# A decoder layer in fp32: GpSimd's weight splits wait at two layer norms, and ScalarE multiplies the index scores by their sign

## What is computed

```python
rel = relu(einsum('bthd,bsd->bths', iq, ik))
score = einsum('bths,bth->bts', rel, iw) * idx_scale      # index scores, causal
_, sel = lax.top_k(score, 256)                            # 256 keys for each query
...                                                       # attention over them, and over a window
h = layer_norm(ALPHA * h + mix, ln1_g, ln1_b)             # LN1
c = memory_cross_attention(h, mem, wq, wk, wv, wo)
h = layer_norm(ALPHA * h + c, ln2_g, ln2_b)               # LN2
h = layer_norm(ALPHA * h + square(relu(h @ w_up)) @ w_down, ln3_g, ln3_b)
```

## Time and profile before

| | us |
|---|---|
| median of 3 runs | 1533.02 (1532.31 to 1533.21) |
| the profiled execution | 1530.0 |
| its span in the trace | 1528.2 |
| PE busy | 1458.5 |
| DVE busy | 1088.0 |
| POOL busy | 756.9 |
| ACT busy | 497.6 |

### The profile page before, as it was taken

One profiled execution on the slowest core, in us unless ns is written; L12 is line 12 of the kernel. 1 busy time (PEld: TensorE's weight loads), 2 busy tenths in 40 slices (PEclk: granted clock), 3 DMA queues, 4 the chain that ended last, 5 costly groups with the idle time before them and its releaser, 6 DMA issues.

```text
span 1528.2 us, 21072 instructions
## 1 busy us (share of the span) xinstructions
PE 1458.5 (95%) x7552; PEld 1243.1 (81%) x7552; DVE 1088.0 (71%) x2097; ACT 497.6 (33%) x1044; POOL 756.9 (50%) x583
## 2 busy tenths in 40 slices
PE   6999898999899999989999899999999999999996
PEld 6877788898899988778887688888888888888885
DVE  7568999787977323964418668787777777777857
ACT  3024488888876621122301111111111111111111
POOL 5341357766700033044312367778676777777612
PEclk9999999999999999999999999999999999999999
DMA  6346156655410042121001002020111112020202
GB/s 240 132 163 173 71 193 198 189 167 179 152 29 15 2 171 77 55 84 55 29 28 56 28 28 83 28 79 32 55 55 56 55 32 80 28 83 1 83 28 83
DMA packets 61479, 128.98 MB, mean 84 GB/s; under 512 B 6976, under 2 KB 34112, under 8 KB 53696
## 3 DMA queue, kind: packets, MB, share of 16 engines
q1 hardware_dynamic: 44352, 100.37, 20.0%
q10 hardware_dynamic: 17024, 27.27, 5.0%
HBM read 100.35 MB, written 27.26 MB: 84 GB/s over the span
## 4 chain that ended last, share of the span: by engine, by line
PE 80%; DVE 12%; issue 2%; ACT 2%; DMA 2%; POOL 1%; ACTq 0%; SPq 0%; DVEq 0%; POOLq 0%
PE banks L872 22%; PE banks L874 22%; PE banks L873 22%; PE banks L1078 4%; PE banks L926 2%; PE banks L927 2%; PE banks L1065 2%; DVE h_buf L2126 2%; PE banks L1034 1%; PE banks L1087 1%; DVE bn L2112 1%; DVE act_lo L2105 1%; DMA u_dram<-stage_out 1%; DVE score L1754 1%; DVE h_buf L2135 1%
## 5 line engine op out<-in xcount | busy, mean ns | idle before, releaser
L782 POOL TENSOR_SCALAR w_hi<-raw 128x512 fp32r<-128x512 f32 x156 | 105.3, 703 | 430.2 <-PE banks L874 278.7
L2251 DVE TENSOR_TENSOR h_buf<-h_buf,banks 128x512 f32<-128x512 f32 x320 | 202.6, 678 | 13.2 <-PE banks L874 9.7
L787 POOL TENSOR_TENSOR w_lo<-raw,w_hi 128x512 fp32r<-128x512 f32 x156 | 209.6, 1379 | 0.0
L872 PE MATMUL banks<-act_hi,w_hi 128*128 128x512 f32 x512 | 200.1, 391 | 1.6 <-DVE act_lo L2105 1.6
L873 PE MATMUL banks<-act_lo,w_hi 128*128 128x512 f32 x512 | 199.9, 390 | 0.0
L874 PE MATMUL banks<-act_hi,w_lo 128*128 128x512 f32 x512 | 199.8, 390 | 0.0
L872 PE MATMUL banks<-w_hi,act_hi 128*128 128x512 f32 x384 | 153.4, 399 | 0.0
L872 PE MATMUL banks<-seven_hi,hid_hi 128*128 128x512 f32 x392 | 152.6, 389 | 0.0
L874 PE MATMUL banks<-seven_hi,hid_lo 128*128 128x512 f32 x392 | 152.5, 389 | 0.0
L873 PE MATMUL banks<-seven_lo,hid_hi 128*128 128x512 f32 x392 | 152.5, 389 | 0.0
L874 PE MATMUL banks<-w_hi,act_lo 128*128 128x512 f32 x384 | 150.7, 392 | 0.0
(11 more groups left out here) (222 smaller groups left out, 3513.5 us busy)
## 6 DMA issues: line engine op xcount, KB each, us to landing
raw<-w_down_dram SPq DMA_DIRECT2D x16, 1024.0 KB, 4.8
raw_up<-w_up_dram SPq DMA_DIRECT2D x14, 1024.0 KB, 4.8
q_tile<-qk_dram SPq DMA_DIRECT2D x176, 64.0 KB, 2.9
qk_dram<-q_hi ACTq DMA_DIRECT2D x28, 256.0 KB, 2.1
qk_dram<-roped ACTq DMA_DIRECT2D x28, 256.0 KB, 2.5
x_raw<-x_t_dram SPq DMA_DIRECT2D x8, 512.0 KB, 8.4
raw<-wk_mem_dram SPq DMA_DIRECT2D x4, 1024.0 KB, 5.3
raw<-wv_mem_dram SPq DMA_DIRECT2D x4, 1024.0 KB, 5.7
```

The costliest lines, as they stand in the source:

```text
L782: pool.tensor_scalar(w_hi[s][:, col], source[:, col], 1.0, 1.0, ALU.mult, ALU.mult)\
L787: pool.tensor_tensor(w_lo[s][:, col], source[:, col], w_hi[s][:, col].bitcast(F32), ALU.subtract).then_inc(w_ready, 1)
L872: pe.matmul(dst, lh, rh, start=(first and n == 0), stop=False)
L2251: ins = dve.tensor_tensor(out, out, ring_m[g % 6][:], ALU.add if way > 0 else ALU.subtract)
```

## The change

GpSimd gets two more waits: ahead of chunk C_G+2 it waits until all 8 tiles of LN1 are done (`ln_done` at NT = 8), and ahead of the first two `form_weights` until all 8 of LN2 are done. The multiplication by the sign goes from VectorE's `prepare` to ScalarE, as an activation `Copy` with the sign as its scale, in the same half, behind the ReLUs of that half and ahead of its counts. Two semaphores carry it: `sign_ready` (VectorE to ScalarE) and `flipped` (ScalarE to those who count). The loop on ScalarE takes a half's ReLUs ahead of its counts; no half has both.

```diff
+FLIPS = [INDEX_HALVES[v] - FIRST_TOPK_TILE for v in sorted(INDEX_HALVES)]
@@ GpSimd, weight chunks
                 pool.wait_ge(raw_in[c % 2], 16 * (c // 2 + 1))
+                if c == C_G + 2:
+                    pool.wait_ge(ln_done, NT)
@@ GpSimd, form_weights
                 if x < 2:
+                    pool.wait_ge(ln_done, 2 * NT)
                     chunk_used(pool, C_MLP - 2)
@@ ScalarE, count_scores
                 if BEFORE[q] is None:
+                    act.wait_ge(flipped, FLIPS.index(c) + 1)
                     act.wait_ge(trial_ready, EARLY_TILES.index(c) + 1)
@@ ScalarE
+            def flip_scores(v):
+                c = INDEX_HALVES[v - 1] - FIRST_TOPK_TILE
+                i = FIRST_TOPK_TILE + c
+                act.wait_ge(sign_ready, FLIPS.index(c) + 1)
+                act.activation(score[i][:], score[i][:], ACT.Copy, scale=sign[:, c:c + 1]).then_inc(flipped, 1)
@@ ScalarE, the loop over the halves
+                    for n in index_own(v):
+                        rectify_scores(n)
+                    if v - 1 in INDEX_HALVES:
+                        flip_scores(v)
                     for q in counts_beside_rope(v):
                         count_scores(q)
-                    for n in index_own(v):
-                        rectify_scores(n)
@@ VectorE, prepare
-                signed = then(dve.tensor_scalar(sign[:, col], negative[:, col], -2.0, 1.0, ALU.mult, ALU.add))
+                dve.tensor_scalar(sign[:, col], negative[:, col], -2.0, 1.0, ALU.mult, ALU.add)\
+                    .then_inc(sign_ready, 1)
-                dve.wait_ge(dve_step, signed)
-                flipped = then(dve.tensor_scalar(score[i][:], score[i][:], sign[:, col], None, ALU.mult))
-                dve.wait_ge(dve_step, flipped)
@@ VectorE, narrow_tally
+                    if c not in found_flipped:
+                        found_flipped.add(c)
+                        dve.wait_ge(flipped, FLIPS.index(c) + 1)
```

More of the change, by code:

```diff
@@ L522, in build_layer @@
         kv_hi_done = sem("kv_hi_done")
+        sign_ready, flipped = sem("sign_ready"), sem("flipped")
         stored = sems("stored", 2)
@@ L1812, in prepare @@
                 dve.wait_ge(dve_step, offsets)
-                dve.wait_ge(dve_step, flipped)
                 dve.memset(trial[:, col], SIGN_BIT + (1 << TOP_BIT)).then_inc(trial_ready, 1)
+            found_flipped = set()
             def select_keys():
                 def narrow_tally(c):
+                    if c not in found_flipped:
+                        found_flipped.add(c)
+                        dve.wait_ge(flipped, FLIPS.index(c) + 1)
                     dve.wait_ge(dve_step, set_at[c])
```

## The result

| | before | after |
|---|---|---|
| median of the runs, us | 1532.66 (1526.5 to 1533.21) | 1518.53 (1516.3 to 1518.72) |
| the profiled execution | 1530.0 | 1518.52 |
| its span in the trace | 1528.2 | 1516.0 |
| ratio of the times | | 0.9917 (0.9892 to 0.9941) |

The changed kernel is faster by 14.1 us at the medians; 13.0 were forecast (1520.0). In the profiled executions it is 11.5 us. Measured twice more, the same kernel came out at 0.9905 (0.9887 to 0.9922) and 0.9905 (0.9885 to 0.9924).

What follows compares the result with a forecast made beforehand. TensorE, busy 95% of the span, was taken as the bound, so time is won only where it waits. LN1 6.6 + LN2 4.0 + sign multiplication 2.4 = 13.0 us, from 1533.0 to 1520.0 us, range 1514 to 1526.

Steps and rivals of the forecast that it cites:

- The wait at LN1: At LN1, holding GpSimd's split removes TensorE gaps of 3.8 and 1.0 us and 1.8 us at half clock: 6.6 us.
- What it puts behind itself: GpSimd's later splits at LN1 move by 10 us, with 20 us left before product 24: cost nothing.
- LN2: At LN2, 3.6 of VectorE's 7 us arrive, low parts following ScalarE's rounding: 4.0 us with the clock fallen.
- one of two cases: Behind LN2, TensorE's clock falls (LN2 gives 4.0 us) or stays up (5.7 us; rival 1517.5 us, chance 0.20).
- The sign part: Index stage: multiplication off VectorE gives 0.68, 0.54, 0.4, 0.8 us for tiles 7, 5, 6, 4: 2.4 us.
- VectorE feels it only in its `flush`, behind `rope_first`: Half 18: ScalarE's counts come 0.9 us later, reaching VectorE only there, so TensorE should not feel it: 0 to 0.9 us.
- the sign of being wrong that was named for it: Half 18: a longer wait of VectorE for ScalarE's counts that moves `rope_first` of the next half.
- The prediction's upper end: Index stage: the multiplication's move gives 4.1 us if one clock fall near 160 us goes too.
- the sign part brings nothing: Rival: ScalarE's counts in half 18 and the late flush give the index-stage gain back: 1522 us, chance 0.15.
- Slower by late splits: Rival: held splits come late at product 24 or the first `seventh` product: 1535.7 us, or 1551; chance 0.03.
- The wait does nothing: Rival: VectorE's stretch at the norms has another cause than GpSimd's splits: 1530.6 us, chance 0.03.
- only instructions with both inputs in SBUF slow down: VectorE beside GpSimd's split at LN1: L2126 goes from 1.27 to 2.31 us, PSUM-reading low parts stay at 1.27 or 1.28.

Runs made afterwards that it cites:

- e3_ln1_wait_only: The kernel before with only GpSimd's wait at chunk C_G+2 (LN1) added: 1524.47 us, ratio 0.9957.
- e6_waits_no_mult: The changed kernel with the sign multiplication left out on both engines, so negative-sign queries get wrong keys: 1513.75 us, ratio 0.9887.
- e9_both_mended: The changed kernel with ScalarE making the high parts of C_G+1 and C_MLP+1, and multiplying tile 4 behind three counts: 1512.35 us, ratio 0.9880.
- e4: The kernel before with only GpSimd's wait in `form_weights` (LN2) added: 1525.60 us, ratio 0.9968.
- e1: The kernel before with GpSimd's two waits alone, the sign multiplication still on VectorE: 1520.13 us, ratio 0.9929.
- e10: The kernel before with GpSimd's two waits alone, measured again beside the changed kernel: 1520.09 us, ratio 0.9921.
- e11: The kernel before with only the sign multiplication moved to ScalarE, measured again beside the changed kernel: 1530.38 us, ratio 0.9986.
- e7_mult_thrice: The kernel before with VectorE multiplying each score tile twice more, by 1.0: 1545.42 us, ratio 1.0097.

## Why the prediction was right, and where it wasn't

**The wait at LN1, 6.6 us.** Held in each step. The low parts of tile 5 were put at 653.06; they start at 653.98 in a profile that is 1.0 us late as a whole. Tile 7's norm was to be done at 658.3 (its three terms give 658.1), ahead of TensorE's wish for it at 660.5; it is done at 659.6, and TensorE transposes at 661.29. Both gaps went, and so did the fall of the clock: 6.8 us in the trace of the wait alone, 6.6 in its times.

**What it puts behind itself, nothing.** GpSimd's hold was worked out as ending at 658.3 with 20 us to spare; it ends at 659.76 (658.8 with the 1.0 us off) with 19.76 us to spare. No wait of TensorE for `w_lo` came at product 24. At LN2 the held `form_weights` are done at 862.35 us and first used at 879.71.

**LN2, 4.0 us.** The step that mattered was that VectorE's 7 us can't all arrive, because TensorE gets to the transposes of tile 6 only behind `up_pair(0)`. The low parts follow ScalarE's rounding by 0.62 us, as said, and the rests are 1.12 and 1.67 us where about 1.1 and 1.6 were said. 4.0 us without the clock. The clock was left as one of two cases, with 1.7 us between them, and both occur. The rule of the Trainium skill that was weighed there ("TensorE: Matmul & The Clock Gate", section "HAM oscillation — how this bites in real kernels", a fall only in long gaps) is not borne out as it stands: behind LN2 the clock fell in four profiles with no rest longer than 1.67 us just ahead.

**The sign part, 2.4 us.** The sum came near, about 2 us as the table below has it, but two of its terms are wrong in opposite directions, so that is in part luck. For tile 7 it took 0.68 us; TensorE's wait fell from 2.69 to 2.05, 0.64. For tile 5 it took 0.54; the wait fell from 2.06 to 1.41 where the clock had fallen near 160 us (the changed kernel and the repeat of the sign part alone), and to 1.53 to 1.57 where it hadn't. For tile 4 it took 0.8, and 0.03 arrived. For tile 6 it took 0.4, all of the wait in the profile before. That wait was short only because TensorE had just run at half clock. `e3_ln1_wait_only` has the multiplication on VectorE and no fall there, and TensorE waited 1.98 us at this place:

```profile
166.87 0.47 PE L928 MATMUL banks<-key_hi,q_tile 128*128 128x512 f32 x1 [1.98 <-DVE score L1756]
```

In the profiles with the sign part and no fall there, the wait is 0.6 us. So at full clock 1.4 of the 1.5 us of tile 6 arrive, and 0.4 behind a fall.

The step that failed is "VectorE feels it only in its `flush`, behind `rope_first`", and the sign of being wrong that was named for it came true: a wait for ScalarE's counts that grew in half 18 and moved `rope_first`. ScalarE's six copies cost it 5.3 us, as said (5). Half 18's counts are late by the copy, 0.83 us against the 0.9 of the prediction, but the first of them is read in the narrow search, ahead of `rope_first`. So the 1.24 us taken off VectorE there came back as 0.93 us of waiting. It could have been worked out from the trace of before: there ScalarE had the first count ready at 189.77 us, and VectorE took it up at 190.67, 0.9 us later. The change brings VectorE there 1.24 us sooner and ScalarE 0.83 us later, 2.1 us together, and 0.9 us of air can't cover them. Leaving the copy out gave the 0.8 us (`e6_waits_no_mult`, 92.4 us where the changed kernel has 93.2 in the table below); moving it behind three counts took TensorE's wait away but gave 0.4 us to the end of the stage (`e9_both_mended`).

What the part is worth in all can be read from profiles in which the clock fell at the same places. From TensorE's wait for tile 7's first sum to its wait for the memory's low part, us:

| falls of the clock between 140 and 170 us | multiplication on VectorE | on ScalarE |
|---|---|---|
| one, near 160 | 94.7 (before) | 93.2 (changed) |
| two, near 143 and near 160 | 95.8, 96.1, 96.1 (`e4`, `e1`, `e10`) | 94.8 (`e11`) |

That is 1.0 to 1.5 us, and with the 0.64 us of tile 7, which lie ahead, 1.7 to 2.1 us.

The prediction's upper end had one fall near 160 us less. Such a fall came in four of the five profiles with neither the sign part nor added work, and in two of the six with the sign part as it stands. But with the multiplication on VectorE it costs nothing: between the waits for tile 7 and for tile 5 went 31.8 us with it (`e1`, `e10`) and 31.8 us without it (`e3`), because TensorE waits for VectorE there in any case. So its absence can't be a gain of its own.

**The first 546 us of the profiled pair.** The end of the index stage (TensorE's wait for the memory's low part) came at 235.53 instead of 239.36 us, 3.8 us earlier. That is more than forecast, and about 1.7 of it are luck: the kernel before had a fall of the clock at 37 us, ahead of all that was changed. Then the way to stage 0 took 310.9 us instead of 306.1. That was the clock in the main: on that way TensorE had half clock for 20.5 us against 13.7, which is 3.4 us of the 4.8. Over the profiles the way is the same: in the five without the sign part it took 305.5 to 312.3 us, 309.0 in the mean, in the six with it 307.2 to 310.9, 308.8 in the mean. The index stage ended at 239.9 us in the mean of the former and at 236.7 in that of the latter, 3.2 us earlier, falls of the clock and all. Executions of one kernel differ in their falls, and I can't say what settles which come. So the rival "the sign part brings nothing" described this pair of profiles, and the others together speak against it: the index stage ends earlier, and the way behind it is no longer. (Its price was added up with the wrong sign: counts that come 0.9 us later take from the gain, 13.0 - 2.4 - 0.9 = 9.7 us, and do not add to it.)

**The other rivals.** Slower by late splits: 19.76 us to spare at LN1, 17.4 us at LN2. The wait does nothing: L2146 is at 1.27 us for every tile of both norms but the two first ones, which still meet a split (2.79 and 2.73 us).

## What to carry to other kernels

Of an instruction that is longer than its twin, ask what GpSimd did just then, and hold that back only where it has air and only past the last step that it hurts: by eight tiles it gave 11 us, by one it cost 7. A step moved to an idle engine delays what is queued behind it there, so look up who reads that queue's next result first. Where a full engine feeds TensorE, as in the index stage here, each microsecond added to it cost its time and some of the clock besides. A wait that is short because the clock had just fallen hides what the engine behind it costs. And parts of 2 us are judged by the waits in the traces, between profiles whose falls of the clock lie at the same places, and by several runs of each, not by one pair of profiles.

## What the runs showed of the hardware that was not expected

Beside a split of GpSimd even VectorE's steps of one element per partition are hurt. The two with two inputs in SBUF go from 0.21 to 1.25 us and from 0.16 to 1.02 us; the step with one such input between them stays at 0.15 us. In a chain of such steps this costs as much as the wide instructions (1.89 us of 3.90 at LN1). The rows of the kernel before had it already; the prediction took the sum and did not look at the single steps. Its sentence that only instructions with both inputs in SBUF slow down is too narrow besides: in `e7_mult_thrice` the two multiplications of tile 6 by 1.0, which read one tile, took 3.17 us beside a split, and the two of tile 7, which are wider, 1.42. The Trainium skill ("GPSIMD Engine Reference", section "8. Key points") names contention for VectorE's instructions with two SBUF inputs or in a two-port mode; the traces agree in kind (1.27 to 2.31 and 2.79 us with two SBUF inputs, 0.62 us for the multiplication of 768 columns against 1.50 us for 896 beside a split, PSUM-reading low parts at 1.27 throughout), and the size is as these rows have it. It goes both ways: GpSimd's own four low parts took 5.04 us in the changed kernel and 7.02 us when they met more of VectorE's steps.

And the clock: with the same rests, 1.12 and 1.67 or 1.68 us, TensorE keeps 2.4 GHz in one kernel (granted 1.00) and falls to 1.2 GHz for part of the next 20 us in another (granted 0.91); behind a rest of 2.36 us both came in one and the same kernel. A fall costs 1.6 to 1.8 us from LN2 to the end (630.6 and 630.4 us with it, 628.8 twice without), and with the multiplication on VectorE nothing near 160 us, where TensorE was going to wait for VectorE anyway.
